# Rows for seven of eight experts: fetched by an indirect DMA and transposed, in place of products with a selection matrix

## The reference

```
def moe(xn, w_router, wg, wu, wd):
    t = xn.reshape(-1, D)
    logits = (t @ w_router).astype(jnp.float32)
    top_vals, top_idx = lax.top_k(logits, TOP_K)
    gates = jax.nn.softmax(top_vals, axis=-1)
    comb = jnp.einsum('nk,nke->ne', gates, jax.nn.one_hot(top_idx, N_EXPERTS, dtype=jnp.float32))
    for e in range(N_EXPERTS):
        y = y + comb[:, e:e + 1].astype(t.dtype) * swiglu(t, wg[e], wu[e], wd[e])
```

## Time and profile before

| | |
|---|---|
| median of 3 runs | 2030.69 us (2030.11 to 2032.65) |
| profiled execution, its own time | 2027.78 us |
| its span, first to last instruction | 2025.4 us |
| mean granted TensorE clock | 0.994 of full speed |
| PE busy | 1983.8 us, 98% of the span |
| DVE busy, ACT busy | 1411.6 us (70%), 1178.4 us (58%) |
| the eight experts | from about 1188 us to the end, some 837 us |

### The profile page before, as it was taken

How to read it: one execution, slowest core, us unless ns; L and a number is a source line. 1 busy time by engine, 2 the same in 40 slices (tenths; PEclk the granted TensorE clock), 3 DMA queues, 4 the chain that set the end, 5 groups by cost and what they waited for, 6 DMA issues and landing times.

```text
span 2025.4 us, 28143 instructions
## 1 busy us (share of the span) xinstructions
PE 1983.8 (98%) x9604; PEld 1661.8 (82%) x9604; DVE 1411.6 (70%) x1711; ACT 1178.4 (58%) x1501; POOL 7.7 (0%) x24
## 2 busy tenths in 40 slices
PE   7989999999999999999999989999999999999998
PEld 6878888888888888888877878888888888888887
DVE  6876654544554454545576779898989898989897
ACT  6656543434433343445465667686767676767675
POOL 1000000000000000000000000000000000000000
PEclk9999999999999999999999999999999999999999
DMA  7544565666566666666654549898989898989896
GB/s 259 182 130 147 181 188 187 191 193 189 187 194 191 188 184 200 188 187 185 193 156 136 187 143 376 294 373 291 376 295 371 298 369 296 369 298 373 300 367 251
DMA packets 135330, 489.31 MB, mean 242 GB/s; under 512 B 15200, under 2 KB 15200, under 8 KB 135104
## 3 DMA queue, kind: packets, MB, share of 16 engines
q1 hardware_dynamic: 134864, 486.64, 71.4%
q0 software_dynamic: 368, 1.41, 0.3%
HBM read 485.90 MB, written 2.10 MB: 241 GB/s over the span
## 4 chain that ended last, share of the span: by engine, by line
PE 94%; ACT 2%; DVE 2%; issue 1%; DMA 1%; SPq 0%; DVEq 0%
PE main L452 28%; PE main L454 28%; PE main L453 28%; PE transpose L762 3%; PE spread L776 1%; PE spread L777 1%; PE transpose L470 1%; DMA raw_pieces<-in_w_in 1%; PE transpose L802 1%; ACT w_high L852 1%; DVE w_low L1165 0%; PE transpose L652 0%; PE spread L514 0%; PE transpose L492 0%; ACT L976 0%
## 5 line engine op out<-in xcount | busy, mean ns | idle before, releaser
L1165 DVE TENSOR_TENSOR w_low<-raw_pieces,w_high 128x1024 fp32r<-128x1024 f32 x920 | 1095.4, 1219 | 441.0 <-ACT w_high L852 436.2
L852 ACT ACTIVATE w_high<-raw_pieces 128x1024 fp32r<-128x1024 f32 x920 | 939.3, 1057 | 230.1 <-DMA raw_pieces<-in_ffn_dense 127.2
L452 PE MATMUL main<-w_high,xT_high 128*128 128x512 f32 (+1 forms) x1920 | 734.4, 382 | 5.7 <-DVE w_low L1165 3.7
L454 PE MATMUL main<-w_high,xT_low 128*128 128x512 f32 (+1 forms) x1920 | 723.8, 377 | 0.0
L453 PE MATMUL main<-w_low,xT_high 128*128 128x512 f32 (+1 forms) x1920 | 722.7, 376 | 0.0
L452 PEld LDWEIGHTS main<-w_high,xT_high 128*128 128x128 f32 x1920 | 363.2, 189 | 70.2 <-issue 4.5
L454 PEld LDWEIGHTS main<-w_high,xT_low 128*128 128x128 f32 x1920 | 362.8, 189 | 66.8
L453 PEld LDWEIGHTS main<-w_low,xT_high 128*128 128x128 f32 x1920 | 363.3, 189 | 62.8
L452 PE MATMUL main<-w_high,hT_high 128*128 128x512 f32 x832 | 328.8, 395 | 0.0
L454 PE MATMUL main<-w_high,hT_low 128*128 128x512 f32 x832 | 324.2, 390 | 0.0
L453 PE MATMUL main<-w_low,hT_high 128*128 128x512 f32 x832 | 324.1, 390 | 0.0
(11 more groups left out here) (199 smaller groups left out, 827.8 us busy)
## 6 DMA issues: line engine op xcount, KB each, us to landing
raw_pieces<-in_ffn_moe SPq DMA_DIRECT2D x528, 512.0 KB, 5.2
raw_pieces<-in_ffn_dense SPq DMA_DIRECT2D x264, 512.0 KB, 3.7
raw_pieces<-in_w_in SPq DMA_DIRECT2D x96, 512.0 KB, 3.6
raw_pieces<-in_w_out SPq DMA_DIRECT2D x32, 512.0 KB, 3.6
x_resid<-in_x SPq DMA_DIRECT2D x4, 512.0 KB, 9.0
out_x<-x_resid SPq DMA_DIRECT2D x8, 256.0 KB, 2.7
token_major<-in_norm_ffn POOLq DMA_DIRECT2D x1, 1024.0 KB, 7.5
heads_scratch<-in_q_norm_dil POOLq DMA_DIRECT2D x2, 64.0 KB, 4.4
```

The lines of the kernel that those rows point to most:

```text
L452: pe.matmul(out_ap, lh[ls], rh[rs], start=first, stop=False)
L454: return pe.matmul(out_ap, ll[ls], rh[rs], start=False, stop=last)
L852: act.activation(WH[:, piece % RING, :], RAWS[:, piece % RING, :], ACT.Copy).then_inc(high_done, 1)
L1165: dve.tensor_tensor(WL[:, piece % RING, :], RAWS[:, piece % RING, :], WH[:, piece % RING, :], ALU.subtract).then_inc(low_done, 1)
```

## The change

For experts 1 to 7 the four `gather` calls give way to this. A copy of the normed tokens is kept in HBM, `xn_rows`, 256 rows of 2048 and one row of zeros. POOL writes it once, behind the router. In iteration 12 PE multiplies `SEL` by the token numbers (less 256), which gives for every slot the number of its token, or 0 for an empty slot; in iteration 14 DVE adds 256 and converts to int32 (`slot_tokens`, so that an empty slot names the row of zeros). POOL then issues an indirect DMA that fetches 128 rows of 8 KB, 1 MB, into `XG`, the place of `GAIN`, which is no longer read. At i = 42, 45, 48 and 51 PE transposes four blocks of `XG` into the same PSUM banks that the products wrote. What ACT and DVE do with them is unchanged, and so are expert 0 and the second pass.

```diff
-E_SELECT = 8
+E_SELECT, E_INDEX = 8, 12
...
+        XG = TOK[:, TILES * D:TILES * D + D]
...
+        TOKEN = sb("token_number", [P, TILES])
+        IDX = sb("slot_tokens", [P, 1], I32)
+        ZERO = sb("zero_row", [P, D // P])
+        ROWS = nc.dram_tensor("xn_rows", (SEQ + 1, D), F32, kind="Internal").ap()
...  (POOL, at the start)
+            pool.iota(TOKEN_I[:, :], [[P, TILES]], base=-SEQ, channel_multiplier=1).then_inc(token_iota, 1)
+            pool.memset(ZERO[:, :], 0.0).then_inc(zero_set, 1)
...  (POOL, at its end)
+            pool.wait_ge(zero_set, 1)
+            pool.dma_start(ROWS[SEQ:SEQ + 1, :].rearrange("o (p n) -> (o p) n", p=P), ZERO[:, :]).then_inc(rows_stored, 16)
+            pool.wait_ge(xn_done, X_BLOCKS)
+            for t in range(TILES):
+                pool.dma_start(ROWS[t * P:(t + 1) * P, :], XN[:, t, :]).then_inc(rows_stored, 16)
+            pool.wait_ge(rows_stored, 16 * (TILES + 1))
+            for e in range(N_EXP - 1):
+                pool.wait_ge(idx_done, e + 1)
+                pool.indirect_dma_start(XG, None, ROWS[:, :], bass.IndirectOffsetOnAxis(ap=IDX[:, 0:1], axis=0)).then_inc(xg_in, 16)
+            pool.wait_ge(xg_in, 16 * (N_EXP - 1))
...  (PE)
+                def slot_tokens(e):
+                    pe.wait_ge(sel_done, e + 2)
+                    pe.wait_ge(sc_free, e * SC_EXPERT + 2)
+                    for t in range(TILES):
+                        ins = pe.matmul(U[0][:, 0:1], SEL[:, t, :], TOKEN[:, t:t + 1], start=t == 0, stop=t == TILES - 1)
+                    ins.then_inc(idx_ready, 1)
+                def gathered(e, count, k, q):
+                    if q == 0:
+                        pe.wait_ge(xg_in, e * 16 + 16)
+                    pe.wait_ge(tp_free, count - 1)
+                    for i in range(4):
+                        c = 4 * q + i
+                        ins = pe.transpose(TP[k % 2][:, i * P:(i + 1) * P], XG[:, c * P:(c + 1) * P], IDN[:, :])
+                    ins.then_inc(tp_ready, 1)
...  (PE, in expert)
+                        if i == E_INDEX and more and n_pass == 0:
+                            slot_tokens(e)
                         if i in E_GATHER and more:
                             q = E_GATHER[i]
-                            if q == 0:
-                                pe.wait_ge(sel_done, e + (N_EXP * n_pass + 2))
-                            gather(e * TP_MORE + (tp_e + tp["gather", q]), tp_e + tp["gather", q], q)
+                            if n_pass == 0:
+                                gathered(e, e * TP_MORE + (tp_e + tp["gather", q]), tp_e + tp["gather", q], q)
+                            else:
...
+                if n_pass == 0:
+                    pe.wait_ge(token_done, 1)
...  (DVE, in masks of layer 0, and in expert)
+                dve.wait_ge(token_iota, 1)
+                dve.tensor_copy(TOKEN[:, :], TOKEN_I[:, :]).then_inc(token_done, 1)
...
+                        if i == E_INDEX + 2 and more and n_pass == 0:
+                            dve.wait_ge(idx_ready, e + 1)
+                            dve.tensor_scalar(IDX[:, :], U[0][:, 0:1], float(SEQ), None, ALU.add).then_inc(idx_done, 1)
```

More of the change, by code:

```diff
@@ L285, in trunk @@
         FLAG = sb("another_pass", [P, 1], I32)
+        TOKEN = sb("token_number", [P, TILES])
+        TOKEN_I = sb("token_number_int", [P, TILES], I32)
+        IDX = sb("slot_tokens", [P, 1], I32)
+        ZERO = sb("zero_row", [P, D // P])
+        ROWS = nc.dram_tensor("xn_rows", (SEQ + 1, D), F32, kind="Internal").ap()
         YH = [HTH[:, 4 * i:4 * i + 4, P:2 * P] for i in range(2)]
@@ L345, in trunk @@
         flag_done = sem("flag_done")
+        zero_set, rows_stored = sem("zero_set"), sem("rows_stored")
+        token_iota, token_done = sem("token_iota"), sem("token_done")
+        idx_ready, idx_done, xg_in = sem("idx_ready"), sem("idx_done"), sem("xg_in")
         sel_done = sem("sel_done")
@@ L804, in expert @@
                             ins.then_inc(tp_ready, 1)
+                        if i == E_INDEX and more and n_pass == 0:
+                            slot_tokens(e)
                         if i in E_GATHER and more:
                             q = E_GATHER[i]
-                            if q == 0:
-                                pe.wait_ge(sel_done, e + (N_EXP * n_pass + 2))
-                            gather(e * TP_MORE + (tp_e + tp["gather", q]), tp_e + tp["gather", q], q)
+                            if n_pass == 0:
+                                gathered(e, e * TP_MORE + (tp_e + tp["gather", q]), tp_e + tp["gather", q], q)
+                            else:
+                                if q == 0:
+                                    pe.wait_ge(sel_done, e + (N_EXP * n_pass + 2))
+                                gather(e * TP_MORE + (tp_e + tp["gather", q]), tp_e + tp["gather", q], q)
                         if i in E_SCATTER:
```

## The result

| | before | after |
|---|---|---|
| median of 4 runs | 2030.40 us (2028.38 to 2032.65) | 2001.47 us (1999.51 to 2003.88) |
| ratio | | 0.9857, 95% interval 0.9845 to 0.9869 |
| profiled execution, its own time, span | 2027.78, 2025.4 us | 2003.88, 2002.1 us |
| one expert, mean of six loops | 103.53 us | 99.26 us |

The kernel is 28.9 us faster. The forecast was 1997, 34.0 us less than before; the time lies in the stated range of 1991 to 2018 and half a microsecond above the 1993 to 2001 that the prediction called the forecast's own. The profiled execution after is the slowest of its four, so its span is not the place to count; the experts are. Seven loops at 4.27 us less would be 29.9 us. Counted directly, from PE's first product of the first loop (1208.27 us before, 1214.22 after) to its first product behind the seventh (1933.09 and 1909.67), they gave 29.4.

What follows compares the result with a forecast made beforehand. PE, busy 98%, bounds the kernel: four calls save 5.36 us per expert, small products cost 0.51, net 4.85, times seven loops 34.0; added waits and stream nothing. 2030.69 - 34.0 = 1996.7, said as 1997; range 1991 to 2018.

Steps and rivals of the forecast that it cites:

- PE gives up what it was said to: Four calls per expert on PE: each falls from 1.78 to 0.44 us, 1.34 less, 5.36 us per expert.
- The small products: Two added one-column float32 products on PE at i = 12: 0.51 us per expert, bounds 0.2 and 0.95.
- The waits that were added: PE at i = 12 and 42, DVE at i = 14: nothing to wait for, index and rows being there early.
- the twin: POOL's broadcast of one row of gains, 1 MB to the same place: landed 7.5 us after issue, POOL busy 0.54.
- The ring follows: Expert weight stream from PE through free slot, load, ACT and DVE back to PE: it keeps up with the faster PE.
- the reserve: Slack of a weight piece between its slot being freed and its use on PE: about 6 of 13.6 us.
- the charge: Delay of the weight stream by one fetch in the gate and up part: 2.7 to 4.4 us.
- PE does not stop: Behind the fetch in each expert: weights stay in time, so PE loses nothing, and the slack grows back.
- rival 2: DVE becomes the bound around the four calls, 20.25 us of work against 20.3: 2 us per expert lost, 2011; chance 0.08.
- Rival 1: DMA engines become the bound in the gate and up part at 350 GB/s: gain only 12 us, 2019; chance 0.10.
- Rival 3: Behind i = 14 the fetch holds up weight loads: at 15 us, 29 us slower, 2060; chance 0.08.
- its threshold: Fetch delay of the weight stream per expert from which the change loses: 6 + 4.85 = 10.9 us.

Runs made afterwards that it cites:

- before_low_last: The kernel before the change, with DVE's low part moved behind everything else of its iteration in the experts, nothing else: 2024.02 us.
- one_fetch: The changed kernel with only the first of the seven fetches, experts 2 to 7 working on expert 1's rows: 1998.78 us.
- blocks_first: The changed kernel with DVE making `h_blocks` ahead of the low part of each expert iteration, not behind it: 1997.97 us.
- products_and_fetch: The changed kernel with the old eight products per call in place of the four transposes, rows fetched and waited for but not used: 2037.37 us.
- low_last: The changed kernel with DVE's low part moved behind everything else of its iteration in the experts: 1991.30 us.
- two_fetches: The changed kernel with each fetch made twice, the second issued when the first has landed: 2023.73 us, ratio to before 0.9969.
- early_fetch: The changed kernel with all experts' indices made once behind expert 0's gathering, and each fetch issued right behind i = 51: 2006.35 us.
- two_fetches_low_last: The changed kernel with each fetch made twice and DVE's low part last in its iteration: 2004.67 us.

## Why the prediction was right, point by point

**PE gives up what it was said to.** Four calls at 1.34 us: the intervals show 3.06 - 1.72 = 1.34, to the digit. The small products: 0.48 for 0.51.

**The waits that were added cost nothing.** No PE wait at i = 12 or at i = 42 shows. The index is made at 1534.27 on DVE without a wait, and the rows land 30 us before use. The fetch took 9.2 to 9.9 us for the twin's 7.5 and POOL 1.67 for 0.54, the part that the prediction had left open.

**The ring follows, and PE does not wait for weights.** Right as said: the reserve was put at 6 us and the charge at 2.7 to 4.4. At i = 27, behind the fetch, the lead of a low part over its use, the mean of six loops, fell from 5.9 to 2.9 us, a charge of 3.0; the least in any loop is 2.7.

**The step that failed** is the conclusion from it, "PE does not stop". I followed the weights round the ring and asked only whether they come in time. What else DVE does in program order between two low parts has no such reserve. The prediction had the wait for `h_blocks` in its first paragraph and took its 3.0 us for nothing; yet that row is the one that says which DVE result is due first. The row is also too small: by the intervals the wait at i = 37 is 0.63 us per loop (2.02 against 1.39 in before_low_last), 4.4 in seven, and a wait of 0.2 us, as at i = 34 after the change, isn't in PE's row at all. one_fetch and blocks_first show what the fetch added to it: 0.42 to 0.46 us per expert, 3 us of the 4.6 by which the seven loops fell short (34.0 forecast, 29.4 measured). That the time still lies in the range is no merit of this step: the range was wide enough for a loss that the sum had put at nothing.

**The rest of the shortfall.** 0.10 us per expert at i = 55 is in one_fetch as well, is missing in products_and_fetch and goes in low_last: a small DVE result again, in the shortened down part. That part is where rival 2 had DVE as full as PE, 20.25 of 20.3 us. Around the four calls it was not:

```profile
1571.60:1592.00 20.40, 20.40 (x99) 16.87 (x98) 17.92 (x20) 13.87 (x17) 0.00 (x0) 1.00 0.93 322
```

17.92 us of 20.40, so the prediction's term was too high, and since the new order takes the 0.10 away with the same work on DVE, it is the order and not the load. In the first loop i = 34 took 2.44 us where the others took 1.66 to 1.83, another 0.6 us once. The last 0.5 us, between the loops' 29.4 and the medians' 28.9, lies ahead of the experts or is scatter. The first call at i = 42 comes at 1269.23 us in the kernel before, at 1271.20 in before_low_last, and between 1271 and 1280 in those with the change. The profiled execution after had a mean granted clock of 0.991, the one before 0.994, and of the four executions after the one at 0.993 is the fastest (1999.51) and the one at 0.991 the slowest (2003.88). With one trace of each this isn't settled.

**Rivals.** Rival 2, DVE as the bound around the four calls: no, see above. Rival 1, the DMA engines as the bound: no. The gate and up part with the fetch in it ran faster than without, 372 GB/s where the earlier trace rows had 350:

```profile
1500.50:1564.00 63.50, 63.48 (x309) 52.94 (x308) 57.66 (x64) 48.25 (x54) 1.67 (x1) 1.00 0.99 372
```

That is 372 GB/s over 63.5 us, above the 358 or so that the Trainium skill ("DMA: Bandwidth & Descriptors", section "Where 436 GB/s comes from") has the HBM side allow and that the prediction weighed; the measurement decides. Rival 3, the fetch holds the stream: no with one fetch. two_fetches shows it at 2 MB, and also that its threshold was wrong: I had 10.9 us of delay before the change loses, and with two fetches, 5.4 us by the prediction's charge of 2.7 each, it has lost 22 of 29 us, because the threshold is that of `h_blocks` and not that of the weights, and because the clock fell behind the waits.

**DVE beside GpSimd.** The low part that started at 1534.34, 0.36 us before the fetch was issued, took 1.22 us; the mean of all went from 1218 to 1223 ns. DVE loses next to nothing, but POOL does wait. Its busy time follows what was left of the low part that ran when the fetch was issued:

| left of the running low part, us | POOL busy with the fetch, us | run |
|---|---|---|
| 0.96 | 1.77 | early_fetch |
| 0.86 | 1.67 | the changed kernel |
| 0.62 | 1.43 | two_fetches_low_last |
| 0.38 | 1.19 | two_fetches |
| none was running | 0.94 | two_fetches |

```profile
1439.88 1.22 DVE L1214 TENSOR_TENSOR w_low<-raw_pieces,w_high 128x1024 fp32r<-128x1024 f32 x1
1441.08 1.22 DVE L1214 TENSOR_TENSOR w_low<-raw_pieces,w_high 128x1024 fp32r<-128x1024 f32 x1
1441.91 1.19 POOL L467 DMA_INDIRECT token_major<-xn_rows,slot_tokens  x1 [90.20 <-DVE slot_tokens L1627]
1554.69 0.94 POOL L467 DMA_INDIRECT token_major<-xn_rows,slot_tokens  x1 [8.13 <-DMA token_major<-xn_rows,slot_tokens]
```

In the four rows with one running the difference is 0.81 us each time. Twice the low part had begun less than 0.05 us before the issue: POOL took 0.94 and the low part 1.27 and 1.29 us, so there DVE was the one to lose, and little. So the late gather that the prediction named as one sign of the rule on shared ports (the Trainium skill, "SBUF — State Buffer", section "Who interferes with whom") is there, and the trace agrees with the rule: 0.7 of the 1.67 us are this wait. With the rows landing 30 us before use it costs nothing here.

## What to carry to other kernels

When a transfer is added to a stream with a reserve, don't stop at whether the stream's own pieces come in time: list everything that stands behind them in program order on the engine that handles them, and ask which of these has the least reserve. Small results that the bound engine waits for belong ahead of work done for later, not behind it; that order alone was worth 10 us here, more than a third of the change. A wait of a few microseconds in total between the bound engine and another is the first place to look, since it tells which result arrives last. Its size is better read from the intervals of the bound engine's own work, and where a wait grows, look at the granted clock behind it before all of the loss is put down to the wait.

## What was not expected of the hardware

- The indirect DMA of 128 rows of 8 KB, 1 MB, landed in 9.2 to 9.9 us in the changed kernel, where a broadcast of one such row to 128 partitions took 7.2 to 7.5. The indirection isn't what makes the difference: the first fetch of early_fetch, at 1204.16, landed in 6.9 us. All engines together moved 286 GB/s during that one, 347 during a fetch of the changed kernel (1534.7 to 1544.5) and 306 to 315 during the broadcasts.
- In two_fetches the granted clock fell to half behind PE's wait at i = 34 in four of seven loops (idle for 2.4 to 2.6 us) and stayed full in the other three (2.1 to 2.5 us).
- Four float32 transposes of 128 x 128 cost PE 0.45 us in the stream, eight float32 products of the same size 1.78 us: 0.11 and 0.22 us each.
- Float32 products with one column cost as much as those with 128 columns: fourteen in a row took 3.04 us in early_fetch, 0.22 each. Both load a stationary side of 128 x 128; that this is what counts is likely and not shown.
